# A decoder's first even norm taken from sums of its parts, and the convolution's activation moved to the gate stage

## The reference

```python
# first block, end
up = causal_depthwise_conv(h2 @ w_up[l], conv_w[l], conv_b[l])
g, v = jnp.split(up, 2, axis=-1)
ff = (jax.nn.gelu(g, approximate=True) * v) @ w_down[l]
x = x + rms_norm(ff, norm_ffn_post[l])

# every layer i of the second block (i = 0 is even, 1 is odd)
h_lat = rms_norm_2(x_lat, norm_g[i]) * (1.0 + sc_l[:, None, :]) + sh_l[:, None, :]
h_ctx = rms_norm_2(x_ctx, norm_g[i]) * (1.0 + sc_c) + sh_c

# odd layer, conformer_conv(val, glu_gate, silu_gate, ...)
u = val * jax.nn.sigmoid(glu_gate)
u = lax.conv_general_dilated(u, ...) + dw_b
u = jax.nn.silu(layer_norm(u, ln_g, ln_b))
return u * jax.nn.silu(silu_gate)
```

## Time and profile before

| what | value |
|---|---|
| median of 3 runs | 1697.06 us |
| profiled execution | 1698.82 us |
| its span | 1697.5 us |
| TensorE busy (PE) | 1651.4 us, 97% |
| TensorE weight loads (PEld) | 1359.8 us, 80% |
| VectorE (DVE) | 993.3 us, 59% |
| ScalarE (ACT) | 736.5 us, 43% |
| GpSimd (POOL) | 652.1 us, 38% |
| mean granted clock of TensorE | 0.996 |

### The profile page before, as it was taken

The page is one execution under the profiler, slowest core; times in us unless marked ns, Lnnn a source line. Parts: engine busy times, 40 slices in busy tenths (PEclk is TensorE's granted clock), DMA queues, the critical chain, the costliest instruction groups (busy, mean ns, idle before and its releaser), DMA issues.

```text
span 1697.5 us, 25757 instructions
## 1 busy us (share of the span) xinstructions
PE 1651.4 (97%) x9979; PEld 1359.8 (80%) x9979; DVE 993.3 (59%) x2018; ACT 736.5 (43%) x1477; POOL 652.1 (38%) x291
## 2 busy tenths in 40 slices
PE   8999999999999999999999999999999999999998
PEld 7789777788888878888878898867777887898686
DVE  4799565543323166555589151566667667996853
ACT  5222355553333354444323444255566326225643
POOL 3766322253234445444464712211112233722341
PEclk9999999999999999999999999999999999999999
DMA  8557212142223423333276322110000432321121
GB/s 248 151 170 202 78 55 75 38 125 75 75 75 105 144 62 100 99 100 99 72 214 189 97 78 73 50 39 14 26 14 14 137 94 82 107 63 57 57 75 50
DMA packets 255160, 156.09 MB, mean 92 GB/s; under 512 B 6017, under 2 KB 251070, under 8 KB 255038
## 3 DMA queue, kind: packets, MB, share of 16 engines
q1 hardware_dynamic: 252238, 147.78, 29.8%
q10 hardware_dynamic: 2800, 6.65, 1.2%
HBM read 152.32 MB, written 2.10 MB: 91 GB/s over the span
## 4 chain that ended last, share of the span: by engine, by line
PE 84%; DVE 11%; issue 2%; ACT 2%; DMA 1%; POOL 1%; ACTq 0%; DVEq 0%
PE ps L819 66%; DVE ps L3182 5%; PE ps L2495 3%; PE ps L2546 3%; PE ps L2509 2%; PE ps L1604 1%; PE ps L1620 1%; DVE mod_sums L1551 1%; PE ps L1566 1%; DVE probsT L2636 1%; PE ps L1612 1%; POOL w_lo L789 1%; DVE h_lo L1138 1%; PE ps L2227 1%; DVE probs L2620 0%
## 5 line engine op out<-in xcount | busy, mean ns | idle before, releaser
L789 POOL TENSOR_TENSOR w_lo<-w_raw,w_hi 128x1024 fp32r<-128x1024 f32 (+2 forms) x220 | 569.4, 2593 | 835.9 <-ACT w_hi L729 835.8
L819 PE MATMUL ps<-h_hi,w_lo 128*128 128x512 f32 x1088 | 437.8, 402 | 8.0 <-POOL w_lo L789 1.6
L819 PE MATMUL ps<-h_hi,w_hi 128*128 128x512 f32 x1088 | 424.5, 390 | 0.0
L819 PE MATMUL ps<-h_lo,w_hi 128*128 128x512 f32 x1088 | 424.2, 390 | 0.0
L819 PEld LDWEIGHTS ps<-h_hi,w_lo 128*128 128x128 f32 x1088 | 204.3, 188 | 57.2 <-issue 5.8
L729 ACT ACTIVATE w_hi<-w_raw 128x1024 fp32r<-128x1024 f32 (+1 forms) x220 | 228.9, 1045 | 39.6 <-PE ps L819 23.1
L819 PEld LDWEIGHTS ps<-h_hi,w_hi 128*128 128x128 f32 x1088 | 204.2, 188 | 44.7
L819 PEld LDWEIGHTS ps<-h_lo,w_hi 128*128 128x128 f32 x1088 | 204.5, 188 | 41.7 <-issue 2.2
L1551 DVE SCALAR_TENSOR_TENSOR mod_sums<-mod_raw,small,mod_sums 128x256 f32<-128x256 f32 x154 | 99.5, 711 | 0.5
L2604 ACT ACTIVATE probs<-probs,small 128x512 f32<-128x512 f32 (+3 forms) x128 | 93.7, 732 | 12.8 <-DVE small L2620 11.5
L2063 ACT ACTIVATE conv<-ps,cols 128x512 f32<-128x512 f32 x44 | 34.3, 779 | 127.4 <-DVE ps L2154 127.4
(11 more groups left out here) (446 smaller groups left out, 3270.3 us busy)
## 6 DMA issues: line engine op xcount, KB each, us to landing
w_raw<-in_w_in SPq DMA_DIRECT2D x56, 512.0 KB, 5.1
mod_raw<-in_mod_w SPq DMA_DIRECT2D x24, 1024.0 KB, 5.8
w_raw<-in_w_up SPq DMA_DIRECT2D x44, 512.0 KB, 3.8
w_raw<-in_od_w_in SPq DMA_DIRECT2D x28, 512.0 KB, 3.7
w_raw<-in_ev_w_in SPq DMA_DIRECT2D x20, 512.0 KB, 3.8
w_raw<-in_w_down SPq DMA_DIRECT2D x16, 512.0 KB, 4.3
...
```

What stands on the lines that cost most here:

```text
L789: POOL.tensor_tensor(wlo[:, p, at:n], raw[:, p, at:n], f(whi[:, p, at:n]), ALU.subtract).then_inc(*chunk_lo.by(c))
L819: ins = PE.matmul(out, l, r, start=first and n == 0, stop=last and n == 2)
```

## The change

Four parts.

- The sum of squares of the new x is no longer taken from the added tiles. x_parts holds the sum of squares of the old x (copied from the norm "h2"). With s the reciprocal root of "ffn", the new sum is that plus 2 s times the sum of x g y (cross_sum, VectorE, L2223 and L2227) plus s² times the sum of g² y² (gain_square, ScalarE, L2110, added by VectorE, L2234). These partial products are made for tiles 0 and 1 with down tile 4, tiles 2 to 4 with down tile 5, 5 and 6 with tile 6, and 7 with tile 7. TensorE sums the two over the features (`pe_sum_parts`, L2015), VectorE puts the total together in five operations on 128x4 (`dve_hx0_square`), ScalarE takes the root.
- TensorE's list after down: three steps of ctx 0, the "ffn" sums, the rest of ctx 0, the spread, the sums of the parts, six steps of ctx 1, the spread "hx0" (now bank 7), the rest. The sums over x tiles and the idle matmuls are gone; the qA tiles run together for six k steps.
- VectorE adds tile t and scales tile t-1 and makes the low part of tile t-2 in turn (`dve_hx0`) in place of two passes. ScalarE issues the second load of the context and the table for Exp later.
- The convolution's activation leaves pairs 8 to 11 of the attention for the start of the gate stage; the fourth `dve_ln_scale` moves from pair 9 to pair 10.

```diff
+    HX0_PARTS = {4: (0, 1), 5: (2, 3, 4), 6: (5, 6), 7: (7,)}
...
     def ctx_back_bank(t):
-        return (6, 4)[t // 2 % 2], t % 2 * CTX
+        return (4, 5)[t // 2 % 2], t % 2 * CTX
...
+        DVE.wait_ge(*rms("h2"))
+        dve_step(DVE.tensor_copy(x_parts[:, 0, :], bank(sum_bank("h2"), NB)))
         dve_rstd("h2")
         DVE.wait_ge(*scale_set(0))
@@ -2014,14 +1989,32 @@
             ins.then_inc(*tile_done.by("dn", c))
...
                 pe_product(1, (c - 3) // 2)
-        run(pe_qa_ctx(0))
+        at = pe_qa_ctx(0)
+        for _ in range(3):
+            next(at)
+        PE.wait_ge(*c_scaled(DT - 1))
         pe_sum_and_last("ffn", "down", (summed("down", DT - 2), last_square("down")))
+        run(at)
+        pe_spread("ffn", 6)
+        pe_sum_parts()
         at = pe_qa_ctx(1)
-        for _ in range(DT // 2):
+        for _ in range(6):
             next(at)
-        pe_spread("ffn", 6)
+        pe_spread("hx0", 7)
         run(at)
         run(pe_qa_ctx(2))
+    def parts_bank(part):
+        return bank(ring_bank("dn", DT - 2), NB, part * NB)
+    def pe_sum_parts():
+        PE.wait_ge(*freed_act("dn", DT - 2))
+        for n, (rows, wait) in enumerate(((cross_sum, summed("cross", DT - 1)), (gain_sum, summed("gain", DT - 1)))):
+            PE.wait_ge(*wait)
+            for b in range(NB):
+                ins = PE.matmul(parts_bank(n)[:, b:b + 1], rows[:, b * P:(b + 1) * P], ones[:, 0:1], start=n == b == 0,
+                                stop=n == 1, skip_group_check=True)
+        ins.then_inc(*sqsum.by("hx0", DT - 1))
...
@@ -2099,17 +2092,36 @@
                 ACTE.wait_ge(*summed("down", u - 2))
...
                 ACTE.activation(ydn[:, u, :], b, ACT.Copy).then_inc(*freed_act.by("dn", u))
+                ACTE.wait_ge(*freed_act("dn", u))
+                gain_square(u)
                 return
-            ACTE.activation(ydn[:, u, :], b, ACT.Copy)
+            act_step(ACTE.activation(ydn[:, u, :], b, ACT.Copy))
             if u >= 2:
...
             ACTE.activation(asq["down"][u % 2][:], b, ACT.Square).then_inc(*freed_act.by("dn", u))
+            for t in HX0_PARTS.get(u, ()):
+                act_after()
+                gain_square(t)
+        def gain_square(u):
+            if u >= 3:
+                ACTE.wait_ge(*summed("gain", u - 2))
+            square = gain_new[u % 2] if u else gain_sum
+            ACTE.activation(square[:], ydn[:, u, :], ACT.Square, scale=col("norm_ffn_post", u)).then_inc(*squared.by("hx0", u))
...
         act_rms("ffn", False, None)
-        ACTE.wait_ge(*tile_done("dn", 23))
+        act_qa_ctx(0)
+        ACTE.wait_ge(*summed("square", "known"))
+        ACTE.activation(statistics("hx0")[0], x_parts[:, 1, :], ACT.Sqrt, scale=1.0 / D_MODEL,
+                        bias=eps).then_inc(*rms.by("hx0"))
+        act_round(first_chunk["qA"] + 3)
         ACTE.dma_start(cin2[:], a["ctx_2"][0].rearrange("(b p) d -> p b d", p=P)).then_inc(again_ctx_landed, 16)
-        act_round(first_chunk["qA"] + 3)
+        ACTE.preload_act_table(ACT.Exp)
+    def act_qa_ctx(u):
+        ACTE.wait_ge(*qa_ctx(u))
+        ACTE.activation(qT3["A"][:, u, 0:CTX], bank(4 + u % 2, CTX), ACT.Copy).then_inc(*qa_ctx_taken.by(u))
...
         rms_, _ = statistics("c0")
@@ -2199,8 +2211,71 @@
                 DVE.wait_ge(*freed_act("dn", u))
...
                     dve_add_square("down", u)
+                for t in HX0_PARTS.get(u, ()):
+                    dve_hx0_parts(t, ydn[:, t, :])
+                if u == DT - 2:
+                    dve_gains(1)
         dve_rstd("ffn")
-        dve_add_normed("ffn", ydn, "norm_ffn_post")
+        dve_hx0()
+    def dve_hx0_parts(u, y):
+        dve_after()
+        dve_step(DVE.scalar_tensor_tensor((cross_new if u else cross_sum)[:], y, col("norm_ffn_post", u), xT[:, u, :],
+                                          ALU.mult, ALU.mult))
+        if u:
+            dve_after()
+            ins = DVE.tensor_tensor(cross_sum[:], cross_sum[:], cross_new[:], ALU.add)
+            if u < DT - 1:
+                dve_step(ins)
+            else:
+                ins.then_inc(*summed.by("cross", u))
+            DVE.wait_ge(*squared("hx0", u))
+            DVE.wait_ge(*(summed("gain", u - 1) if u > 1 else squared("hx0", 0)))
+            DVE.tensor_tensor(gain_sum[:], gain_sum[:], gain_new[u % 2][:], ALU.add).then_inc(*summed.by("gain", u))
+    def dve_hx0_square():
+        s = statistics("ffn")[1]
+        new = x_parts[:, 1, :]
+        DVE.wait_ge(*sqsum("hx0", DT - 1))
+        DVE.wait_ge(*rstd("ffn"))
+        dve_step(DVE.tensor_tensor(new, parts_bank(1), s, ALU.mult))
+        dve_after()
+        dve_step(DVE.scalar_tensor_tensor(new, parts_bank(0), 2.0, new, ALU.mult, ALU.add))
+        dve_after()
+        dve_step(DVE.tensor_tensor(new, new, s, ALU.mult))
+        dve_after()
+        dve_step(DVE.tensor_tensor(new, new, x_parts[:, 0, :], ALU.add))
+        dve_after()
+        DVE.tensor_scalar(new, new, 0.0, None, ALU.max).then_inc(*summed.by("square", "known"))
+    def dve_hx0():
+        DVE.wait_ge(*spread("ffn"))
+        for t in range(DT + 2):
+            if t < DT:
+                if t >= 2:
+                    DVE.wait_ge(*x_added("ffn", t - 2))
+                dve_step(DVE.scalar_tensor_tensor(wtmp["ffn"][t % 2][:], ydn[:, t, :], col("norm_ffn_post", t), bank(6),
+                                                  ALU.mult, ALU.mult))
+                dve_after()
+                DVE.tensor_tensor(xT[:, t, :], xT[:, t, :], wtmp["ffn"][t % 2][:], ALU.add).then_inc(*x_added.by("ffn", t))
+            if t == 0:
+                dve_hx0_square()
+            if t == 1:
+                dve_rstd("hx0")
+                DVE.wait_ge(*spread("hx0"))
+                DVE.wait_ge(*gains_set(1))
+            if 1 <= t <= DT:
+                k = t - 1
+                DVE.wait_ge(*x_added("ffn", k))
+                if k >= 3:
+                    DVE.wait_ge(*n_lo("hx0", k - 3))
+                DVE.scalar_tensor_tensor(wtmp["hx0"][k % 3][:], xT[:, k, :], modulated_gain(0, 0)(k), bank(7), ALU.mult,
+                                         ALU.mult).then_inc(*n_scaled.by("hx0", k))
+            if t >= 2:
+                k = t - 2
+                DVE.wait_ge(*n_hi("hx0", k))
+                DVE.scalar_tensor_tensor(hlo[:, k, :], wtmp["hx0"][k % 3][:], shift(0, 0)(k), f(hhi[:, k, :]), ALU.add,
+                                         ALU.subtract).then_inc(*n_lo.by("hx0", k))
...
@@ -2269,28 +2344,17 @@
         ins.then_inc(*v_taken.by(x_))
...
     def pe_even_projections():
-        at = pe_qa_ctx(3)
+        run(pe_qa_ctx(3))
         views = [chunk_views(first_chunk["qA"] + u) for u in range(4)]
-        for t in range(DT):
-            PE.wait_ge(*squared("hx0", t))
-            for b in range(NB):
-                ins = PE.matmul(bank(7, 1, b), wsq["hx0"][t % 2][:, b * P:(b + 1) * P], ones[:, 0:1],
-                                start=t == 0 and b == 0, stop=t == DT - 1, skip_group_check=True)
-            ins.then_inc(*sqsum.by("hx0", t))
-            if t < 4:
-                next(at)
-                next(at)
         PE.wait_ge(again_ctx_landed, 16)
-        PE.wait_ge(*x_added("ffn", DT - 1))
+        PE.wait_ge(*qa_ctx_taken(2))
         pe_ctx_back(0)
...
         PE.wait_ge(*qa_ctx_taken(3))
-        pe_spread("hx0", 5)
         pe_ctx_back(2)
...
             wait_bank("qA", u)
-        pe_idle(7, views[3][0].rearrange("p k n -> p (k n)"), 0)
...
             hi, lo = views[u]
...
+        together = DT - 2
+        for k in range(together):
             PE.wait_ge(*n_lo("hx0", k))
...
                 qa_step(u, k)
@@ -2307,7 +2372,7 @@
                 PE.wait_ge(*fm_act("c", 2 * u + 1))
...
                 pe_ctx_back(2 * u + 5)
-            for k in range(DT // 2, DT):
+            for k in range(together, DT):
                 PE.wait_ge(*n_lo("hx0", k))
                 qa_step(u, k)
@@ -2375,20 +2440,14 @@
         return pairs_
...
     def act_even_projections():
-        def take_ctx(u):
-            ACTE.wait_ge(*qa_ctx(u))
-            ACTE.activation(qT3["A"][:, u, 0:CTX], bank(4 + u % 2, CTX), ACT.Copy).then_inc(*qa_ctx_taken.by(u))
-
-        def ready(t):
-            ACTE.wait_ge(*x_added("ffn", t))
-            if t in (3, 6):
-                take_ctx(t // 3 + 1)
-
-        take_ctx(0)
-        take_ctx(1)
-        act_squares("hx0", xT, ready)
-        act_rms("hx0", False)
-        act_apply("hx0", hhi, shift(0, 0), lambda t: act_ctx_back(t - 4) if t >= 4 else None)
+        def beside(t):
+            if t in (2, 3):
+                act_qa_ctx(t)
+            elif t >= 4:
+                act_ctx_back(t - 4)
+        act_qa_ctx(1)
+        act_apply("hx0", hhi, shift(0, 0), beside)
...
             if u < 2:
@@ -2440,10 +2499,6 @@
         ins.then_inc(*gains_set.by(layer))
...
     def dve_even_projections():
-        dve_gains(1)
-        dve_rstd("hx0")
```

(22 more changed lines are left out.)

45 lines of the change are left out of this document (10 added, 35 removed).

## The result

The changed kernel takes 1686.63 us (median of 4 runs, 1685.5 to 1687.51), the kernel before 1696.76 beside it: ratio 0.9934, with 95% confidence 0.9923 to 0.9946. That is 10.1 us less. The forecast was 1684.6 (1681.5 to 1689.5). The profiled execution took 1687.51, its span 1686.2, against 1698.82 and 1697.5: 11.3 less, where the steps of the forecast summed to 12.5.

A forecast was written before the change was run, and what follows sets the result against it. TensorE, 84% of the span, was taken to bound the kernel. 9.8 + 3.8 - 0.6 - 0.5 = 12.5 off the profiled 1698.8 gives 1686.3, 1684.6 for the median; 8-in-10 range 1681.5 to 1689.5.

The forecast's parts named there:

- The norm, 9.8: Between down projection and qA: the first norm needs no added tile, so qA starts at 997.1, not 1006.9; 9.8 us off.
- The step on ctx_again: First norm: the load is issued behind the second root at about 988.5, lands at 995.2, TensorE asks at 996.2; 1.0 cover.
- rival 2: First norm: longer wait, from late small operations or 3 us lost at half clock; gain 7, not 12.5: 1690; 12%.
- Rival 4: Slower: the clock falls in the sums at about 984 and does not come back in qA; 1714 us; 3%.
- w_lo in tile 5, 0.6: Down stage: four more VectorE operations may hold off GpSimd's w_lo; TensorE loses 0 to 1.7 us, 0.6 taken.
- Attention, 3.8: Odd attention, pairs 8 to 11: the activation leaves; gain 0 to 4.4 us, 3.8 taken.
- Gate stage, 0.5: Gate stage: VectorE's last ln_silu beside GpSimd's w_lo may delay the last o_lo; loss 0 to 1.5 us, 0.5 taken.
- rival 1: Port lock bites everywhere: 1.7 at w_lo, 1.1 to 1.5 in gate stage, about 1.8 at last gain add; 1688.5; 14%.
- o_lo of gate tile 3 before wo3's step 3: Sign for being right, gate stage: the last o_lo is ready before wo3's first tile reaches its k step 3, 1644.6.

The follow-up runs named there:

- add_first: The changed kernel, but VectorE adds all eight tiles before it scales the first for the norm, not in turn: 1693.38 us, ratio 0.9973.
- add_first_ctx: add_first with ScalarE's copies of context query tiles 2 and 3 moved ahead of its first h_hi: 1692.27 us, one run.
- six_close: The changed kernel with six unused VectorE products more, close together, ahead of the first cross product of down tile 4: 1691.9 us, one run.
- the four kernels: The changed kernel with unused VectorE products ahead of the first cross product: six close together, six each behind the last, twelve narrow, eight mostly in place: 1691.9, 1692.1, 1693.26, 1692.93 us.
- act_only: The kernel before with only the convolution's activation moved from attention to the gate stage: 1696.24 us, ratio 0.9988.

## Why the prediction was right, step by step

**The norm, 9.8: right, 10.0.** qA 18.41 after ctx 0 (18.5 predicted). Small operations 0.20 each, 0.24 taken; the wait 0.26, 0.7 taken; h_lo every 2.70, 2.8 taken. The step on ctx_again was wrong in place: ScalarE's queue issued it at 986.33, ahead of the rounding, not behind it at 988.5, and it took 5.6, so its cover was 3.3 and not 1.0. What the prediction didn't say, and the two add_first runs show, is that the parts are the smaller half: without the turn 6.2 to 8.0 of the 10.0 are gone; of the 6.2, 2.6 are the clock. That is near the 3 us that rival 2 put on it. Rival 4's clock that doesn't come back was not seen: in add_first_ctx it fell behind a wait of 3.3 and was 0.94 again over 1004 to 1007. In the changed kernel, with a wait of 0.26, it stayed at 1.00.

**w_lo in tile 5, 0.6: 0.** The lower end of the term came true: GpSimd got in directly behind the add, w_lo ended at 939.5, before TensorE asks, and the next VectorE products lasted 2.33 to 2.77 in place of 0.75. The Trainium skill, page "SBUF — State Buffer", section "SBUF: two separate sides", says that the port pair which the two engines share is held for a whole instruction; the trace agrees. But I had put this down to the short stop between two products, and six_close, with no stop, shows that none is needed. What the added work does is another thing: it makes VectorE late for its reciprocals (L2208), which release ScalarE's context rows, and behind them in ScalarE's list its eviction of tile 5, its rounding, w_lo, and then TensorE. VectorE (first four rows) and ScalarE, changed kernel:

```profile
937.68 2.33 DVE L2223 SCALAR_TENSOR_TENSOR cross_sum<-y_down,cols,x_T 128x512 f32<-128x512 f32 x1
940.05 2.77 DVE L2223 SCALAR_TENSOR_TENSOR cross_new<-y_down,cols,x_T 128x512 f32<-128x512 f32 x1
942.85 2.76 DVE L2227 TENSOR_TENSOR cross_sum<-cross_sum,cross_new 128x512 f32<-128x512 f32 x1
...
946.13 0.21 DVE L2208 RECIPROCAL statistics<-statistics 128x1 f32<-128x1 f32 x2
```
```profile
946.32 2.38 ACT L2139 ACTIVATE ctx_in<-ctx_in,small,statistics 128x1024 f32<-128x1024 f32 x2 [10.65 <-DVE statistics L2208]
```

By the four kernels that chain ended 0.7 to 0.8 before TensorE asked: an estimate, their delay less their wait. The prediction had not followed it.

**Attention, 3.8: 3.3 in this profile, 3.6 in act_only.** The mechanism was right; four pairs took 16.9. But 1.4 us of VectorE's time there was one product of 2737 ns that met GpSimd's mask add. With the norm's part in front it no longer did, attention was 1.5 shorter with the activation still in it, and the removal was worth 2.0. The two parts don't add up, and that the whole came out near 3.8 owes something to luck.

**Gate stage, 0.5: 1.5.** This is the step that failed in size. The wait was of the kind described (o_lo of tile 3, behind a product that stands behind w_lo, 1.1 of TensorE's time), which was rival 1 at this place; I had put the product beside that w_lo myself and still taken a value below the middle. The rest up to 1.5 is how that wait is counted (see the two matmuls above). So of the signs named for being right, "o_lo of gate tile 3 before wo3's step 3" failed. Of rival 1's other two places neither cost TensorE anything: at w_lo of tile 5 it was 0, and VectorE's last gain add came at 980.54, 0.35 ahead of GpSimd's w_lo at 980.89, and took 0.68.

**Not foreseen:** 1.1 at the first pair of odd attention, by the clock; its cause is open.

So 12.5 was forecast; 10.0 + 3.3 - 1.5 - 1.1 - 0.2 = 10.5 is what the table gives behind ctx 0, and the medians say 10.1. Too little was taken off for the gate stage (1.0) and nothing for the clock (1.1); the 0.6 for w_lo that didn't come offset part of it, which is luck in the sum.
